# Forty-eight tokens of a PEER kernel's last chunk are taken out of the dense U product, and VectorE's searches, dots and masks are laid out anew around it

## The chip, the cores and the metric

The kernel runs on one NeuronCore of a Trainium2 chip. TensorE (PE) multiplies, VectorE (DVE) and ScalarE (ACT) do element-wise work, GpSimd (POOL) issues the gathers, SyncE (SP) issues most loads. All engines run their own instruction streams and meet at semaphores. The metric is the device time of one execution in microseconds; the kernel before takes 1597.27 us (median of three runs, 1597.15 to 1597.89).

## The reference

512 tokens of 1024 channels go through a gated short-convolution and pooling mixer, then through a PEER layer, which is where the change lies:

```python
q = (xf @ w_query).reshape(t, 8, 2, 128)
scores = einsum('thpk,hpnk->thpn', q, sub_keys)       # 8 heads, 2 halves, 128 keys
v1, i1 = top_k(scores[:, :, 0], 16)
v2, i2 = top_k(scores[:, :, 1], 16)
cand = v1[..., :, None] + v2[..., None, :]
best, pos = top_k(cand.reshape(t, 8, 256), 16)
experts = e1 * 128 + e2                                # 128 experts for a token, of 16384
gates = softmax(best)
a = gelu(einsum('cd,ced->ce', x, expert_u[experts])) * gates
out = einsum('ce,ced->cd', a, expert_v[experts])
```

All is float32 at the borders. The kernel makes each float32 product from three products of float32r parts (high by high, high by low, low by high), which is the origin of the names `w_hi`, `w_lo`, `xn_hi`, `xn_lo`.

## The kernel before, in words

**Tiles.** All weights come as tiles of 128 x 1024 numbers (512 KB), 344 in all: 32 for the input projection, 4 for the pool, 32 for the gates, 8 for `w_out`, 16 for the query, 128 for U, 128 for V. Four slots hold them. SP loads `w_raw` once the slot's `w_lo` is done, ACT makes `w_hi` (`split_weight`, L683) once PE has finished the tile four places earlier, DVE makes `w_lo` (L1272), PE multiplies (`tile_product`, L1019: eight blocks of three matmuls, 24 in all).

**Who computes what in PEER.** The 128 tokens of chunk 0 never enter the dense products: DVE takes their 128 expert rows of U each by gather (POOL, L597, a ring of four 512 KB buffers, one row for each of 128 tokens) and dots them with `x_tok` (L1666), and later adds gated rows of V into `out_tok` (L1895). The last `EXTRA` = 32 tokens of chunk 3 are taken out of the dense U product as well: 128 experts for a token are one more kind of gathered row, with 16 partitions for a token and eight tokens (`SHARED`) in a group (L1673), each row against `x_extra`, which holds a group's x. The other 352 tokens get the dense product of x with all 16384 rows of U: 128 tiles of 24 matmuls with 352 columns (`DENSE`, `DU`). V takes 384 tokens, in matmuls of 512 columns.

**Order in the U stage** (U tiles 0 to 127). While PE multiplies the query tiles and then U tiles, DVE searches the top 16 of each head (`search`, L1544), one chunk and two heads at a call, and decodes expert numbers. Between the pieces of a search stand a few `u_split` (L1534), the DVE step that frees a bank and makes the `w_lo` of the tile four further on (for half of tiles 4 to 39 `w_lo` comes from DRAM and DVE only signals). `hold` between two pieces makes DVE wait until the piece before is written. The tables `SEARCHES`, `DOTS_BEFORE`, `DOTS_ROUND` and `DOTS_PLAIN` (L134 and on) say how many splits and dots stand where. Retrieval ends before the split of U tile 52.

**Masks.** From U tile 60 to 107 run six rounds of eight tiles. In a round DVE writes four mask groups of 16 tokens (`mask_half`, L1803): one 128 x 2048 tensor of e1 lanes and, in the next place, two (three for the `EXTRA` tokens) of gated e2 columns, one group for two tiles, besides one `w_lo` and `DOTS_ROUND` dots for a tile. PE turns them into gates by 128 x 128 products (L1199), half a mask group (16 matmuls) after each tile: it needs mask group n after tile 2n of the stage. The second half of group n is written before the split at tile 2n - 1. ACT copies the results (L878), two groups of four tokens behind each tile, and stores them to `g_dram`, 2 MB for four tiles. Steps 27 to 30 (16 tiles) are plain: U tiles and dots alone. What dots are then left run in the first V tiles; from V tile 37 on, DVE adds 128 rows of V, spread evenly to the end.

The lines that say this most briefly:

```python
DOTS_ROUND = (1, 1, 1, 2, 1, 1, 1, 2)
for q in (2 * b, 2 * b + 1):                      # PE, after u_tile b
    if q % 4 == 0:
        pe.wait_ge(masks_ready, MASKS_PER_ROUND * s + (q // 4 + 1))
if q >= ROW_SLOTS:                                # POOL: the ring of four
    pool.wait_ge(rows_used, q - ROW_SLOTS + 1)
```

Of the kernel before, what the change touches and what calls it, by code (L numbers as in the profile page):

```python
# [75 lines left out]
EXTRA = 32  # L76
# [18 lines left out]
EXP_AT = 54  # L95
# [33 lines left out]
def is_early(step, b):  # L129
# [4 lines left out]
SEARCHES = (((3, 1, 1, 0), 0, 2), ((2, 1, 0, 1), 1, 2), ((2, 1, 1, 0), 0, 2), ((2, 0, 1, 1), 1, 2),  # L134
            ((2, 1, 0, 1), 0, 2), ((1, 1, 1, 0), 2, 2), ((2, 1, 0, 1), 0, 2), ((1, 1, 1, 1), 2, 2),
            ((2, 1, 1, 0), 0, 0), ((2, 1, 0, 1), 2, 0))
BEFORE_FIRST = EXP_AT - 2
DOTS_BEFORE = (1, 1, 1, 2, 1, 1, 1)
DOTS_ROUND = (1, 1, 1, 2, 1, 1, 1, 2)
DOTS_PLAIN = (2, 2, 1, 2)  # L140
DOTS_TOPK = sum(dots for _, _, dots in SEARCHES)
# [4 lines left out]
X_STORED, X_LOADED, X_AT_ONCE = 6, 10, 2  # L146
assert EXTRA_SHOWN + 2 < EXTRA_FIRST and EXTRA % MASKED == 0
# [70 lines left out]
class Chain:  # L218
# [23 lines left out]

    def hold(self, carrier):


        self.wait()
        self.engine.sem_inc(carrier, 1)


def build(nc, x_t, params_d, w_in_d, pool_d, gate_d, w_out_d, query_d, keys_d, u_d, v_d, u_rows, gain_d, out_d,  # L250
          act_dram, g_dram, index_dram, extra_dram, x_rows_dram, early_dram):
    ctx = ExitStack()
    with ctx:
# [71 lines left out]
        top_v = rest("top_v", [P, 2, 2, TOPK])  # L325
        top_i = rest("top_i", [P, 2, 2, 2, 2, TOPK], U32)
        less = rest("less", [P, 4, KEYS])
        cand = rest("cand", [P, 2, CANDS])
        cand_less = rest("cand_less", [P, 2, CANDS])
# [5 lines left out]
        x_last = rest("x_last", [P, D])  # L335
# [4 lines left out]
        extra_t = small("extra_t", [P, EXTRA])  # L340
        extra_rows = small("extra_rows", [P, PAIRS])
        gate_x = small("gate_x", [P, EXTRA_PARTS, EXTRA], BF16)
# [3 lines left out]
        beside_xn = MemoryMap(nc, xn_at)  # L346
        x_extra = [beside_xn(f"x_extra{k}", [P, NB, T])[:, :, 0:GT] for k in range(X_BUFFERS)]
        assert beside_xn.at <= scratch_at
# [19 lines left out]
                 for k, at in enumerate(mask_regions)]  # L368
        masks_x = [MemoryMap(nc, at)(f"masks_x{k}", [P, 1 + EXTRA_PARTS, MASKED // 2, KEYS, 2], BF16)
                   for k, at in enumerate(mask_regions)]  # L370
        g_build.at += 2 * (1 + EXTRA_PARTS) * MASKED * KEYS
# [210 lines left out]
        def _(pool):  # L582
# [30 lines left out]
            def load_extra(t):  # L613

                g, at = t // SHARED, t % SHARED * SPREAD
                pool.dma_start(x_extra[g % X_BUFFERS][at:at + SPREAD],
                               x_rows_dram[t:t + 1, :].broadcast_to([SPREAD, D])
                               ).then_inc(x_extra_loaded[g % X_BUFFERS], 16)
# [15 lines left out]
            for q in range(U_ROWS):  # L634
# [38 lines left out]
        def _(act):  # L673
# [224 lines left out]
            act.activation(act_out[:, :, DU:], ones[:, 0:SLOTS * EXTRA].rearrange("p (b t) -> p b t", b=SLOTS), ACT.Copy  # L898
# [30 lines left out]
            for b in range(SLOTS // 2, SLOTS):  # L929
                gelu_tile(ONEHOT_AT - 1, b)  # L930
# [1067 lines left out]
```

## Time and profile before

| what | value |
|---|---|
| median of three runs | 1597.27 us |
| the profiled execution, its own time | 1597.16 us |
| its span, first to last instruction | 1595.4 us |
| PE busy | 1587.8 us (100%) |
| DVE busy | 1289.7 us (81%) |
| ACT busy | 701.6 us (44%) |
| POOL busy | 426.2 us (27%) |
| granted TensorE clock | full (1.000) |
| DMA moved | 459.85 MB, mean 288 GB/s |

The span in 40 slices shows DVE at 7 or more tenths from the thirteenth slice on, and the DMA engines at 9 tenths from the 20th to the 39th, at 333 to 414 GB/s. The chain that ended last is 98% PE. A matmul's own time in a row is from issue to its last result; matmuls overlap, so the pace is the distance of two starts. VectorE's instructions overlap a little too: 1.22 us for a 128 x 1024 operation, with the next one 1.14 us after its start.

The U stage runs from 521 to 1064 us, the mask rounds in it from 752 to 990 us, the V stage from 1067 to 1590 us.

### The profile page before, as it was taken

To read this page: it belongs to the slowest core of one execution; us is meant where nothing else is said; L and a number is where in the kernel's file an instruction comes from. 1 tells how busy PE (TensorE), PEld (TensorE's weight loads), DVE (VectorE), ACT (ScalarE), POOL (GpSimd) and SP (SyncE) were. 2 spreads that over 40 slices of the span, in tenths; PEclk is the share of its full clock that TensorE was granted. 3 is DMA by queue.
4 is the path that set the end of the run, shared out by engine and by line. 5 is a ranking of instruction groups with operands and counts; after the bars stand their busy time and mean duration, and the time that the engine had idled before them with its cause. 6 is when DMAs were issued, how large, how long until landed. Compare 5 with 4: busy or idle time off the path is not lost.

```text
span 1595.4 us, 25473 instructions
## 1 busy us (share of the span) xinstructions
PE 1587.8 (100%) x8590; PEld 1403.7 (88%) x8590; DVE 1289.7 (81%) x2373; ACT 701.6 (44%) x936; POOL 426.2 (27%) x373
## 2 busy tenths in 40 slices
PE   9999999999999999999999999999999999999998
PEld 8888888888888999999999999998888888888886
DVE  6967833334578888988999998779998999999997
ACT  5444533333333433335776776443334333333334
POOL 1011100000000112203353322434445555455451
PEclk9999999999999999999999999999999999999999
DMA  5477632323322699968999999999999999999994
GB/s 214 143 250 239 234 106 96 101 92 100 111 82 78 231 337 318 325 205 281 333 386 410 406 389 379 407 356 373 390 413 387 413 414 394 410 407 397 404 358 162
DMA packets 150237, 459.85 MB, mean 288 GB/s; under 512 B 16336, under 2 KB 47104, under 8 KB 148512
## 3 DMA queue, kind: packets, MB, share of 16 engines
q1 hardware_dynamic: 82080, 231.08, 39.4%
q0 software_dynamic: 47888, 172.15, 28.5%
q10 hardware_dynamic: 20208, 55.94, 9.3%
q8 instruction: 22, 0.36, 0.1%
q14 instruction: 39, 0.32, 0.1%
HBM read 402.78 MB, written 56.33 MB: 288 GB/s over the span
## 4 chain that ended last, share of the span: by engine, by line
PE 98%; ACT 1%; DVE 1%; DMA 1%; issue 0%; SPq 0%; DVEq 0%; ACTq 0%
PE bank L1036 20%; PE bank L1038 20%; PE bank L1037 20%; PE bank L1223 11%; PE bank L1224 11%; PE bank L1222 11%; PE bank L1199 3%; PE bank L1102 1%; DMA h_t<-x_t 1%; PE bank L1236 0%; ACT w_hi L689 0%; DVE w_lo L1275 0%; PE bank L1081 0%; PE bank L1083 0%; PE bank L1082 0%
## 5 line engine op out<-in xcount | busy, mean ns | idle before, releaser
L689 ACT ACTIVATE w_hi<-w_raw 128x1024 fp32r<-128x1024 f32 x347 | 365.9, 1056 | 349.9 <-PE bank L1224 238.9
L1036 PE MATMUL bank<-xn_hi,w_hi 128*128 128x352 f32 (+1 forms) x1472 | 510.4, 347 | 0.0
L1275 DVE TENSOR_TENSOR w_lo<-w_raw,w_hi 128x1024 fp32r<-128x1024 f32 x329 | 401.6, 1221 | 130.8 <-ACT w_hi L689 126.9
L1037 PE MATMUL bank<-xn_lo,w_hi 128*128 128x352 f32 (+1 forms) x1472 | 504.7, 343 | 0.0
L1038 PE MATMUL bank<-xn_hi,w_lo 128*128 128x352 f32 (+1 forms) x1472 | 504.7, 343 | 0.0
L597 POOL DMA_INDIRECT rows<-u_rows,expert x128 | 152.8, 1193 | 610.3 <-DVE expert L1703 353.9
L1222 PE MATMUL bank<-w_hi,a_hi 128*128 128x512 f32 x768 | 298.8, 389 | 0.0
L1224 PE MATMUL bank<-w_hi,a_lo 128*128 128x512 f32 x768 | 298.8, 389 | 0.0
L1223 PE MATMUL bank<-w_lo,a_hi 128*128 128x512 f32 x768 | 298.8, 389 | 0.0
L1038 PEld LDWEIGHTS bank<-xn_hi,w_lo 128*128 128x128 f32 x1472 | 276.7, 188 | 17.7
L1037 PEld LDWEIGHTS bank<-xn_lo,w_hi 128*128 128x128 f32 x1472 | 276.9, 188 | 17.4 <-issue 0.2
L1036 PEld LDWEIGHTS bank<-xn_hi,w_hi 128*128 128x128 f32 x1472 | 276.7, 188 | 17.3 <-issue 0.2
L597 POOL DMA_INDIRECT rows<-v,expert x128 | 189.6, 1481 | 175.6 <-DVE out_tok L1895 161.9
L1222 PEld LDWEIGHTS bank<-w_hi,a_hi 128*128 128x128 f32 x768 | 144.1, 188 | 30.0
L1224 PEld LDWEIGHTS bank<-w_hi,a_lo 128*128 128x128 f32 x768 | 144.1, 188 | 29.9
L1223 PEld LDWEIGHTS bank<-w_lo,a_hi 128*128 128x128 f32 x768 | 144.1, 188 | 29.9
L1895 DVE SCALAR_TENSOR_TENSOR out_tok<-rows,dots,out_tok 128x1024 f32<-128x1024 f32 x128 | 163.9, 1280 | 6.9 <-DMA rows<-v,expert 3.4
L1666 DVE SCALAR_TENSOR_TENSOR rows<-rows,x_tok 128x1024 f32<-128x1024 f32 x128 | 154.0, 1220 | 17.0 <-DMA rows<-u_rows,expert 16.7
L864 ACT ACTIVATE act_out<-bank 128x352 f32<-128x352 f32 x112 | 52.1, 465 | 210.3 <-PE bank L1038 203.8
L962 ACT ACTIVATE a_hi<-a_f 128x384 fp32r<-128x384 f32 x128 | 66.9, 523 | 77.2 <-DVE a_f L1876 76.9
L878 ACT ACTIVATE g_sb<-bank 128x512 f32<-128x512 f32 x96 | 100.7, 1164 | 0.0
L1882 DVE TENSOR_TENSOR a_lo<-a_f,a_hi 128x384 fp32r<-128x384 f32 x128 | 70.5, 551 | 0.0
(239 smaller groups left out, 1486.1 us busy)
## 6 DMA issues: line engine op xcount, KB each, us to landing
w_raw<-u SPq DMA_DIRECT2D x128, 512.0 KB, 6.7
w_raw<-v SPq DMA_DIRECT2D x128, 512.0 KB, 7.1
g_dram<-g_sb ACTq DMA_DIRECT2D x12, 2048.0 KB, 10.9
g_in<-g_dram SPq DMA_DIRECT2D x84, 256.0 KB, 9.0
act_dram<-act_out ACTq DMA_DIRECT2D x54, 352.0 KB, 5.7
act_in<-act_dram SPq DMA_DIRECT2D x54, 352.0 KB, 8.5
w_raw<-gate SPq DMA_DIRECT2D x32, 512.0 KB, 3.3
w_raw<-w_in SPq DMA_DIRECT2D x31, 512.0 KB, 3.8
```

Source lines behind the costliest of these rows:

```text
L597: pool.indirect_dma_start(out=rows[:, slot, :], out_offset=None, in_=table.rearrange("a p d -> (a p) d"), in_offset=bass.IndirectOffsetOnA ...
L689: act.activation(w_hi[:, slot, :], w_raw[:, slot, :], ACT.Copy).then_inc(hi_done, 1)
L878: act.activation(g_sb[:, k, :, t:t + TOKENS_PER_GROUP].rearrange("p e t -> p t e"), bank[4 + q % SLOTS][:].rearrange("p (t e) -> p t e", e ...
L1036: pe.matmul(out, hi, x_hi, start=k == 0, stop=False)
L1037: pe.matmul(out, hi, x_lo, start=False, stop=False)
L1038: last = pe.matmul(out, lo, x_hi, start=False, stop=k == NB - 1)
L1222: pe.matmul(out, a_h, v_hi, start=False, stop=False)
L1223: pe.matmul(out, a_h, v_lo, start=False, stop=False)
L1224: return pe.matmul(out, a_l, v_hi, start=False, stop=final)
L1275: dve.tensor_tensor(w_lo[:, slot, :], w_raw[:, slot, :], w_hi[:, slot, :].bitcast(F32), ALU.subtract).then_inc(lo_done, 1)
L1666: dve.scalar_tensor_tensor(rows[:, slot, :], rows[:, slot, :], 1.0, x_tok[:], ALU.mult, ALU.mult, accum_out=dots[:, r:r + 1]).then_inc(row ...
L1895: dve.scalar_tensor_tensor(out_tok[:], rows[:, slot, :], dots[:, ds(r)], out_tok[:], ALU.mult, ALU.add).then_inc(v_rows_used, 1)
```

## The change

- **Tokens.** `EXTRA` is 48 instead of 32. The dense U product takes 336 columns instead of 352, six instead of four groups of eight tokens go by gathered rows (16 more rows, 176 instead of 160), and three instead of two mask groups have three parts.
- **Searches.** `search` takes two chunks. Each piece is issued for chunk s = 0 and then for s = 1, and `hold_at` waits on the mark of the same chunk's piece before. Retrieval ends before the split of U tile 44 instead of 52.
- **x of the row dots.** `x_extra` is a contiguous 128 x 1024 tensor, loaded by one DMA for a group of eight tokens instead of eight DMAs of one token each into a tensor with gaps (512-byte pieces).
- **Mask groups.** PE takes all 32 matmuls of a group (48 with three parts) after every second tile instead of 16 after every one: it needs group n after tile 2n + 1. ACT copies four groups of four tokens after every second tile.
- **Dots.** 10 in retrieval (16 before), 22 from there to the masks (8), 11 in each of six rounds (10), 28 in the plain steps (28), 50 in V (48). The sum is 176 (160). Rows of V begin at V tile 41 instead of 37. The three turning products of e1, e2 and gates come after U tile 51 instead of 57.

```diff
-EXTRA = 32
+EXTRA = 48
-MASKS_X = EXTRA // MASKED
+MASKS_X = -(-EXTRA // MASKED)
+THREE_PARTS = MASKED * MASKS_X
-DOTS_BEFORE = (1, 1, 1, 2, 1, 1, 1)
-DOTS_ROUND = (1, 1, 1, 2, 1, 1, 1, 2)
+DOTS_FIRST = 1
+DOTS_SEARCH = (1, 1, 1, 2)
+DOTS_DECODE = (1, 1, 1, 1)
+BEFORE_FIRST = 44
+DOTS_BEFORE = (1, 1, 1, 2, 1, 2, 1, 1, 2, 1, 2, 1, 1, 2, 2, 1)
+DOTS_ROUND = (1, 1, 2, 1, 1, 2, 1, 2)
...
+            def load_extra(g):
+
+                pool.dma_start(x_extra[g % X_BUFFERS][:],
+                               x_rows_dram[g * SHARED:(g + 1) * SHARED, :].unsqueeze(1).broadcast_to([SHARED, SPREAD, D])
+                               ).then_inc(x_extra_loaded[g % X_BUFFERS], 16)
...
+                kind, r = u_row(q + SHARED - ROW_SLOTS)
+                if kind and r % SHARED == 0 and r >= X_BUFFERS * SHARED:
+                    load_extra(r // SHARED)
...
-                    for q in (2 * b, 2 * b + 1):
+                    for q in range(2 * (b - 1), 2 * (b + 1)) if b % TILES_PER_MASK == TILES_PER_MASK - 1 else ():
...
+            def mask_groups(s, n, last_round):
+                pe.wait_ge(masks_ready, MASKS_PER_ROUND * s + (n + 1))
+                for q in range(SLOTS * n, SLOTS * (n + 1)):
+                    pe.wait_ge(g_copied, GROUPS_PER_ROUND * s + (q + 1))
...
+                    if b % TILES_PER_MASK == TILES_PER_MASK - 1:
+                        mask_groups(s, b // TILES_PER_MASK, last_round)
...
-            def search(c, i, at, splits):
+            def search(chunks, i, splits):
...
+                for s in both:
+                    for k, u, half in rows_of:
+                        chain.did(dve.max(top_v[:, s, half, u, 0:8], row(s, k)))
+                    done[s] = chain.mark()
+                for s in both:
+                    chain.hold_at(done[s], held)
+                    for k, u, half in rows_of:
+                        chain.did(dve.max_index(index(s, half, u)[:, 0:8], top_v[:, s, half, u, 0:8], row(s, k)))
+                        chain.did(dve.match_replace(less[:, s, k, :], top_v[:, s, half, u, 0:8], row(s, k), LOWEST))
+                    done[s] = chain.mark()
+                    splits[s]()
```

**VectorE at the start of a search.** Before: one chunk (MAX finds eight of the largest, x4 is four calls; `w_lo` is the split of a weight tile).

```order
L1554 MAX top_v<-scores 128x8 x4
L1557 MAX_INDEX top_i<-top_v,scores 128x8
L1558 MATCH_REPLACE less<-top_v,scores 128x128
L1557 MAX_INDEX top_i<-top_v,scores 128x8
L1558 MATCH_REPLACE less<-top_v,scores 128x128
L1557 MAX_INDEX top_i<-top_v,scores 128x8
L1558 MATCH_REPLACE less<-top_v,scores 128x128
L1557 MAX_INDEX top_i<-top_v,scores 128x8
L1558 MATCH_REPLACE less<-top_v,scores 128x128
L1275 TENSOR_TENSOR w_lo<-w_raw,w_hi 128x1024
L1562 MAX top_v<-less 128x8 x4
L1565 MAX_INDEX top_i<-top_v,less 128x8 x4
```

VectorE of the changed kernel, in the second part of a search's first half:

```order
L1576 MATCH_REPLACE less<-top_v,scores 128x128
L1289 TENSOR_TENSOR w_lo<-w_raw,w_hi 128x1024
L1582 MAX top_v<-less 128x8 x8
L1587 MAX_INDEX top_i<-top_v,less 128x8 x4
L1590 TENSOR_TENSOR cand<-top_v 128x2x64
L1590 TENSOR_TENSOR cand<-top_v 128x2x48
L1587 MAX_INDEX top_i<-top_v,less 128x8 x4
L1590 TENSOR_TENSOR cand<-top_v 128x2x64
```

Eight MAX of two chunks stand together, and the second chunk's four lie between the first chunk's four and the operation that reads them.

**TensorE in the first mask round.** Before, after a U tile:

```order
L1038 MATMUL bank<-xn_hi,w_lo 128x352
L1190 ISA
L1191 ISA
L1199 MATMUL bank<-masks_127 128x128 x8
L1191 REGISTER_ALU
L1199 MATMUL bank<-masks_127 128x128 x8
L1026 REGISTER_ALU
L1036 MATMUL bank<-xn_hi,w_hi 128x352
```

TensorE in the first mask round of the changed kernel, after the second U tile:

```order
L1050 MATMUL bank<-xn_hi,w_lo 128x336
L1192 ISA
L1194 ISA
L1202 MATMUL bank<-masks_124 128x128 x8
L1194 REGISTER_ALU
L1202 MATMUL bank<-masks_124 128x128 x8
L1194 REGISTER_ALU
L1202 MATMUL bank<-masks_124 128x128 x8
L1194 REGISTER_ALU
L1202 MATMUL bank<-masks_124 128x128 x8
L1038 REGISTER_ALU
L1048 MATMUL bank<-xn_hi,w_hi 128x336
```

Thirty-two mask products stand in a row where there were sixteen, and one U tile more lies ahead of them.

**GpSimd beside the row gathers.** Before (16x8x128 is one token's x):

```order
L597 DMA rows<-u_rows,expert_extra 128x1024 x12
L616 DMA x_extra_118<-x_rows_dram 16x8x128 x2
L597 DMA rows<-u_rows,expert_extra 128x1024
L616 DMA x_extra_118<-x_rows_dram 16x8x128 x2
L597 DMA rows<-u_rows,expert_extra 128x1024
```

GpSimd of the changed kernel at the same place:

```order
L613 DMA rows<-u_rows,expert_extra 128x1024 x12
L631 DMA x_extra_128<-x_rows_dram 128x1x1024
L613 DMA rows<-u_rows,expert_extra 128x1024 x8
L631 DMA x_extra_129<-x_rows_dram 128x1x1024
```

One load of 512 KB stands ahead of eight gathers where eight loads of 64 KB stood between them.

## Rows read from the trace of the kernel before

**Rows 1.** The page, part 1: engine, busy us (share of the span), instructions.
```profile
PE 1587.8 (100%) x8590; PEld 1403.7 (88%) x8590; DVE 1289.7 (81%) x2373; ACT 701.6 (44%) x936; POOL 426.2 (27%) x373
```

**Rows 2.** Waits of TensorE, whole span: us in total, times, longest.
```profile
PE bank L1058 <- POOL p_pad L585: 1.0, 1, 1.0
```

**Rows 3.** Timeline of TensorE in the U stage: start us, us, instruction.
```profile
599.70 0.32 PE L1036 MATMUL bank<-xn_hi,w_hi 128*128 128x352 f32 x1
...
603.54 0.32 PE L1036 MATMUL bank<-xn_hi,w_hi 128*128 128x352 f32 x1
```

**Rows 4.** Timeline of TensorE in the V stage.
```profile
1199.76 0.39 PE L1222 MATMUL bank<-w_hi,a_hi 128*128 128x512 f32 x1
...
1203.84 0.39 PE L1222 MATMUL bank<-w_hi,a_hi 128*128 128x512 f32 x1
```

**Rows 5.** Chain that ended last, beside the first mask products: start us, us.
```profile
756.85 0.94 PE bank L1199 x16
757.79 0.21 PE bank L1036
```

**Rows 6.** Chain that ended last, a group with three parts.
```profile
969.69 1.40 PE bank L1199 x24
```

**Rows 7.** Timeline of VectorE in a search.
```profile
703.73 0.88 DVE L1554 MAX8 top_v<-scores 128x8 f32<-128x128 f32 x4
704.75 0.09 DVE L1557 MATCH_VALUE_LOAD top_i<-top_v,scores 128x8 f32 x1
```

**Rows 8.** Waits of VectorE while it searches, 445 to 728 us.
```profile
DVE w_lo L1275 <- ACT w_hi L689: 15.1, 11, 3.1
```

**Rows 9.** Timeline of VectorE in a mask round.
```profile
884.43 0.42 DVE L1755 TENSOR_TENSOR low_hot<-iota_key,e_low 128x512 f16<-128x512 f16 x1
...
887.77 2.35 DVE L1775 TENSOR_TENSOR masks<-gated_hot,low_hot 128x2048 f16<-128x2048 f16 x2
...
902.59 0.41 DVE L1755 TENSOR_TENSOR low_hot<-iota_key,e_low 128x512 f16<-128x512 f16 x1
```

**Rows 10.** Timeline of ScalarE at one U tile.
```profile
749.21 0.47 ACT L864 ACTIVATE act_out<-bank 128x352 f32<-128x352 f32 x1 [1.90 <-PE bank L1038]
749.57 1.05 ACT L689 ACTIVATE w_hi<-w_raw 128x1024 fp32r<-128x1024 f32 x1
```

**Rows 11.** Waits of VectorE in the mask rounds, 752 to 990 us.
```profile
DVE w_lo L1275 <- ACT w_hi L689: 7.7, 19, 2.9
DVE rows L1673 <- DMA rows<-u_rows,expert_extra: 5.0, 4, 2.5
```

**Rows 12.** Waits of VectorE in the plain steps, 990 to 1064 us.
```profile
DVE rows L1666 <- DMA rows<-u_rows,expert: 14.5, 13, 2.7
```

**Rows 13.** Stretches: us, busy us of each engine (instructions), PEclk, DMA share, GB/s.
```profile
752.00:990.00 238.00, 238.00 (x1980) 231.62 (x1979) 224.48 (x296) 165.10 (x196) 81.67 (x75) 1.00 1.00 381
990.00:1064.00 74.00, 74.00 (x466) 73.98 (x465) 56.91 (x81) 31.32 (x56) 35.26 (x30) 1.00 1.01 399
...
1230.00:1560.00 330.00, 330.00 (x1458) 273.25 (x1457) 313.27 (x361) 126.83 (x163) 171.90 (x117) 1.00 1.02 400
```

**Rows 14.** DMA issues, 752 to 990 us: count, KB each, us to landing.
```profile
rows<-u_rows,expert POOLq DMA_INDIRECT x31, 9.8
rows<-u_rows,expert_extra POOLq DMA_INDIRECT x28, 11.6
```

**Rows 15.** DMA issues, 1230 to 1560 us.
```profile
rows<-v,expert POOLq DMA_INDIRECT x117, 7.4
```

**Rows 16.** Timeline of VectorE in the V stage.
```profile
1314.87 2.67 DVE L1895 SCALAR_TENSOR_TENSOR out_tok<-rows,dots,out_tok 128x1024 f32<-128x1024 f32 x2
1317.45 0.56 DVE L1876 TENSOR_TENSOR a_f<-act_in,g_in 128x384 f32<-128x384 f32 x1
...
1319.52 1.28 DVE L1895 SCALAR_TENSOR_TENSOR out_tok<-rows,dots,out_tok 128x1024 f32<-128x1024 f32 x1
1320.72 0.55 DVE L1876 TENSOR_TENSOR a_f<-act_in,g_in 128x384 f32<-128x384 f32 x1
```

More of the change, by code:

```diff
@@ L94 @@
 ONEHOT_AT = 15
-EXP_AT = 54
+TURN_AT = 13
 ROUND = 2
@@ new lines, in search @@
+                for s in both:
+                    chain.hold_at(done[s], held)
+                    for k, u, half in rows_of:
+                        chain.did(dve.max(top_v[:, s, half, u, 8:16], less[:, s, k, :]))
+                    done[s] = chain.mark()
+                for s in both:
+                    chain.hold_at(done[s], held)
+                    for k, u, half in rows_of:
+                        chain.did(dve.max_index(index(s, half, u)[:, 8:16], top_v[:, s, half, u, 8:16], less[:, s, k, :]))
+                    for first, count, width, start in ((0, TOP_A, TOPK, 0), (TOP_A, TOPK - TOP_A, LOW_B, WIDE)):
+                        part = [P, 2, count, width]
+                        chain.did(dve.tensor_tensor(
+                            cand[:, s, :, start:start + count * width].rearrange("p u (a b) -> p u a b", a=count),
+                            top_v[:, s, 0, :, first:first + count].unsqueeze(3).broadcast_to(part),
+                            top_v[:, s, 1, :, 0:width].unsqueeze(2).broadcast_to(part), ALU.add))
+                    done[s] = chain.mark()
+                    splits[2 + s]()
@@ new lines, in search @@
+                for s in both:
+                    chain.hold_at(done[s], held)
+                    for u in range(2):
+                        chain.did(dve.max(top(s, u)[:, 0:8], cand[:, s, u, :]))
+                    done[s] = chain.mark()
+                for s in both:
+                    chain.hold_at(done[s], held)
+                    for u in range(2):
+                        chain.did(dve.max_index(place(s, u)[:, 0:8], top(s, u)[:, 0:8], cand[:, s, u, :]))
+                        chain.did(dve.match_replace(cand_less[:, s, u, :], top(s, u)[:, 0:8], cand[:, s, u, :], LOWEST))
+                    done[s] = chain.mark()
@@ new lines, in search @@
+                splits[4]()
+                for s in both:
+                    chain.hold_at(done[s], held)
+                    for u in range(2):
+                        chain.did(dve.max(top(s, u)[:, 8:16], cand_less[:, s, u, :]))
+                    done[s] = chain.mark()
+                splits[5]()
+                for s in both:
+                    chain.hold_at(done[s], held)
+                    for u in range(2):
+                        chain.did(dve.max_index(place(s, u)[:, 8:16], top(s, u)[:, 8:16], cand_less[:, s, u, :]))
```

304 lines of the change are left out of this document (131 added, 173 removed).

## The prediction

> **What bounds the kernel now.** Read the busy times first: PE is busy for the whole span [rows 1], and the longest of its three waits is 1.0 us, at the very start [rows 2]. So the time is PE's own sum, and nothing else counts until PE waits for it. The second look is for PE's pace. In the U stage 24 starts take 3.84 us, 160 ns for a matmul of 352 columns [rows 3]; in V 18 starts take 4.08 us, 226.7 ns for 512 columns [rows 4]. The third look is for who is close behind PE: in the mask rounds DVE is busy 224.5 of 238 us, in V 313.3 of 330, and the DMA engines are full in both (share 1.00 and 1.02) [rows 13]. That is where a faster PE runs into something.
>
> **PE's own sum.** The two paces differ by 66.7 ns for 160 columns, 0.417 ns a column. Sixteen columns fewer: 6.67 ns, 153.3 ns a matmul, and for 128 tiles x 24 = 3072 matmuls 20.5 us less. The third mask part for 16 more tokens is 16 products of 1.40/24 = 58 ns [rows 6]: 0.9 us more. The first U matmul behind mask products takes 0.21 instead of 0.16 us on the chain [rows 5]; there are 24 such places instead of 48: 1.2 us less. PE's sum is 20.8 us less. The profiled execution took 1597.16 us (1.8 us outside its span), the median is 0.1 above it: 1576.5 if PE never waits. Gathers and DVE must serve a PE that is faster, with 16 rows more; so each stage is looked at.
>
> The weight load could be a floor here: at 352 columns PEld is busy for 73.98 of 74 us [rows 13], and then narrower matmuls win nothing. Against it: from 352 to 512 columns the pace grows by just one column each 2.4 GHz cycle, at the full granted clock, which a floor that held at 352 would bend; and mask products follow each other in 58 ns, loads included, though of 16 bit. The Trainium skill (TensorE: Matmul & The Clock Gate, section "LDWEIGHTS (loading the stationary operand)") gives the load as columns over 1.2 GHz, 107 ns for 128. By it there is no floor at 153 ns and the 20.5 us stand; no row here shows a 32-bit load as a bound.
>
> **Retrieval** (445 to 728 us). It now ends 8 tiles earlier, and 44 U tiles are 0.16 us shorter: DVE has 8 x 3.84 + 44 x 0.16 = 37.8 us less. It saves 8 `w_lo` of 1.14 (9.1) and 6 dots of 1.15 (6.9). A `hold` costs about 0.22 us: four MAX end at 704.61, and the next starts at 704.75, and loses the 0.08 overlap that it would have had [rows 7]. Of seven in a search some four have no `w_lo` in front; paired, all are covered: 16 x 4 x 0.22 = 14. Sum 30; the other 8 come from the 15.1 us in which DVE waits for `w_hi` [rows 8]. It fits with 7 us in hand; cost 0, and up to 8 if the pairs save only half.
>
> **From retrieval to the masks.** 16 tiles x 1.14 + 22 x 1.15 = 43.5 us, and about 9 for the gates and mask group 0 (an estimate from operations as in [rows 9]), in 58.9 us of PE. It fits, but the gates and group 0 (about 6 us) come in one piece near the end, so DVE enters the rounds some 3 us behind (estimate, 0 to 6).
>
> **Mask rounds.** Half a round of DVE without a wait took 902.59 - 884.43 = 18.16 us [rows 9], a round 36.3, with an eleventh dot 37.5. PE's round was 8 x (3.84 + 0.94 + 0.05) = 38.6 and becomes 8 x (3.68 + 0.94) + 0.2 = 37.2. So DVE, which had 2.3 us a round to spare, now lacks 0.3: 2 us in six rounds, and 2 more for the third part of one more group (one operation of 1.14 [rows 9] and its small ones). Gathers: the ring of four must turn in 4/11 of 37.2 = 13.5 us (15.4 before). A row of `expert_extra` lands 11.6 us after its issue, the others 9.8 [rows 14]; with dot and issue 13.1 and 11.3. Spare is 0.4 us where it was 2.3, and with 2.3 DVE lost 5.0 us in four waits [rows 11]. I take 8 us; 0 if the single `x_extra` loads lighten the queue, 20 if landings grow by a microsecond. What is allowed: DVE can begin a split 1.5 us after PE's tile (ACT's 1.4 [rows 10] and a signal). Mask group n stands before split 2n - 1 and PE asks for it after tile 2n + 1, two tiles and a group of products later: 7.36 + 1.87 - 1.5 = 7.7 us of room (3.3 in the order before). 3 + 2 + 2 + 8 = 15 against 7.7 gives 7; some gather waits fall where DVE would wait for `w_hi` anyway (7.7 us of that now [rows 11]), so I take 4, from bounds of 0 and 16.
>
> **Plain steps.** 28 dots and 16 `w_lo` are 50.4 us, row waits 14.5 [rows 12]: 65 us against PE's 58.9. DVE falls 6 us further behind, having won back 3.4 at the two places of the last round that have no masks; room is three tiles less 2.7, 8.3 us. I take 2 us, from 0 to 6.
>
> **V.** The other steps take 1319.52 - 1317.45 = 2.07 us, one row 1.20, a pair 2.58 [rows 16]. 128 rows over 86 tiles instead of 90 are 1.49 a tile: 2.07 + 1.87 = 3.94 us of 4.08 (3.85 before). The ring may take 10.97 us and takes 7.4 [rows 15] + 1.6. Cost 0, while landings stay.
>
> Sum: -20.8 + 4 + 2 = -14.8, that is **1582.5 us**.
>
> **Rivals.**
> *All is covered.* `x_extra` in one piece makes short packets go away, landings shorten, DVE stays inside its room: waits under 3 us, 1577. For it: room in the masks more than doubles. Against: the ring's 0.4 us.
>
> *The DMA engines set the pace.* The stretch of the masks moved 238 us x 381 GB/s = 90.7 MB at a share of 1.00, the plain one 74 x 399 = 29.5 [rows 13]. Six rows and an x group add 3.7, the narrower `act_out` takes 0.5 off: 93.9 MB in 238 - 8 = 230 us are 408 GB/s, then 29.5 in 71.4 are 413. Seen over such lengths are 381 to 400. If the masks stay at 381, they take 246.5 us, 16.5 longer than PE needs: 1576.5 + 16 = 1592.5. For it: the full share. Against: 400 in V at the same share, so share alone is no ceiling. The Trainium skill (DMA: Bandwidth & Descriptors, section "Where 436 GB/s comes from") puts the fabric's ceiling at 435 GB/s, by which 413 passes, and gives about 358 for one core's HBM; the 400 of the rows is above that one already.
>
> *Slower: the ring of V.* Two more dots run in V, and the 128 rows of V crowd into 86 tiles. From a landing of 9.4 us on, the ring turns slower than 10.97 and the whole V stage follows it. At 10.3 us, between this and what the mask rounds show for gathers [rows 14], it turns in 11.9: 32 x 11.9 = 381 us where 351 are given, 30 us more: 1612. For it: mask rounds show 9.8 to 11.6 at the same share. Against: V asks for hardly more bytes, and its row landed in 7.4.
>
> *Nothing is won.* A floor of the weight load: 128 tiles as long as now, 1597.
>
> **Chances.** Forecast 0.52 (1579.5 to 1587), all covered 0.22, DMA pace 0.14, no gain 0.04, slower 0.08. This kernel's measurement can tell about 0.2%, 3.2 us, from no change. Faster 0.52 + 0.22 + 0.13 = 0.87, same 0.05, slower 0.08. The range 1576 to 1593 leaves out the slower case, the floor and the worse half of the DMA case, some 0.19.
>
> **What the new profile should show.** Starts of U matmuls 153.3 ns apart (160 or more would be the floor). 24 groups of 32 or 48 mask products, the row behind at 0.21. PE's waits: next to none before 752 us, some 4 us for `masks` or `w_lo` in the rounds, the later the more, 2 in the plain steps, none in V. DVE at 97% or more in the rounds, its waits for `w_hi` there gone and those for rows of `expert_extra` near 8 us. Retrieval over at about 690 us. The forecast is wrong if PE waits in retrieval or V, if DVE keeps waiting for `w_hi` in the rounds, or if landings move by more than a microsecond either way.

## The result: slower by 1.7%, and the profile after

The changed kernel takes 1622.65 us (median of four runs, 1620.14 to 1631.82) against 1597.49 for the kernel before: a ratio of 1.0168, 95% interval 1.0148 to 1.0188. Forecast were 1582.5 us, and slower had a chance of 0.08. The profiled execution took 1620.67 us. Its page says of PE, and of all DMA packets:

```profile
PE 1579.9 (98%) x8606; PEld 1394.2 (86%) x8606; DVE 1300.5 (80%) x2411; ACT 701.8 (43%) x936; POOL 443.6 (27%) x365
DMA packets 153534, 467.63 MB, mean 289 GB/s; under 512 B 17296, under 2 KB 48080, under 8 KB 151808
```

PE was busy for the whole span before [rows 1]; now it waits. Its waits over the whole span (us in total, times, longest), beside [rows 2]:

```profile
PE bank L1202 <- DVE masks L1800: 15.1, 7, 4.7
PE bank L1048 <- DVE w_lo L1289: 12.8, 10, 4.7
PE bank L1202 <- DVE masks_x L1800: 2.6, 1, 2.6
```

What PE's own work was forecast to win is there. In the U stage two starts that lie 24 matmuls apart (start, duration):

```profile
785.61 0.32 PE L1048 MATMUL bank<-xn_hi,w_hi 128*128 128x336 f32 x1
789.29 0.32 PE L1048 MATMUL bank<-xn_hi,w_hi 128*128 128x336 f32 x1
```

3.68 us for 24 is 153.3 ns, where [rows 3] had 160. So the loss must be waits. Here is one from its root to PE. First GpSimd's queue, then DVE, then PE, in that stretch (start, duration, and in brackets the idle time before and what ended it):

```profile
775.05 0.66 POOL L631 DMA_DIRECT2D x_extra<-x_rows_dram  x1 [2.90 <-DVE rows L1704]
776.01 1.07 POOL L613 DMA_INDIRECT rows<-u_rows,expert_extra  x1 [0.30 <-issue]
```

```profile
786.00 1.22 DVE L1289 TENSOR_TENSOR w_lo<-w_raw,w_hi 128x1024 fp32r<-128x1024 f32 x1
793.17 1.23 DVE L1704 SCALAR_TENSOR_TENSOR rows<-rows,x_extra 128x1024 f32<-128x1024 f32 x1 [5.95 <-DMA rows<-u_rows,expert_extra]
794.32 2.35 DVE L1800 TENSOR_TENSOR masks<-gated_hot,low_hot 128x2048 f16<-128x2048 f16 x2
```

```profile
796.80 3.59 PE L1202 MATMUL bank<-masks 128*128 128x128 f16 x32 [4.59 <-DVE masks L1800]
800.15 0.63 PE L1048 MATMUL bank<-xn_hi,w_hi 128*128 128x336 f32 x1
800.58 0.48 PE L1049 MATMUL bank<-xn_lo,w_hi 128*128 128x336 f32 x1
...
808.08 2.01 PE L1202 MATMUL bank<-masks 128*128 128x128 f16 x32
```

The gather issued at 776.01, right behind a 512 KB load of `x_extra`, feeds the dot of 793.17: 17.2 us, where [rows 14] had 11.6. DVE stands still for 5.95 us, its masks are late, and PE waits 4.59 us for them. Then comes a second price: the same 32 mask products take 3.59 us instead of 2.01, and the U starts behind them are 0.43 and 0.28 us apart instead of 0.153. The granted clock in those stretches (columns as in [rows 13]):

```profile
796.00:800.00 4.00, 3.20 (x31) 3.21 (x32) 4.00 (x5) 2.13 (x3) 0.59 (x2) 0.50 0.84 276
804.00:808.00 4.00, 4.00 (x28) 3.96 (x26) 4.00 (x6) 1.40 (x2) 1.14 (x1) 1.00 1.00 417
```

0.50 is the lower level, 1.2 GHz, right behind a wait; it is back at 2.4 GHz a few us later. The wait cost 4.59 us. Of the 6.9 us at half clock around it (794.3 to 801.2) PE was busy for 4.40, so the slow start cost about half of that, 2.2 us more.

Every wait of over 3 us has this root. The loads for groups 2 to 5 are issued at 745.70, 775.05, 809.43 and 842.49; the first or second gather behind each reached its dot after 15.0, 17.2, 15.3 and 15.6 us, and PE's waits of 4.72, 4.59, 4.75 and 3.78 us follow. The loads of groups 0 and 1 stand ahead of the first extra rows:

```profile
691.94 0.69 POOL L631 DMA_DIRECT2D x_extra<-x_rows_dram  x1 [0.59 <-DVE rows L1697]
...
700.60 0.66 POOL L631 DMA_DIRECT2D x_extra<-x_rows_dram  x1 [0.57 <-DVE rows L1697]
```

Between 698 and 766 us DVE waits 21.0 us for rows, 10.9 of them for the three issued between and behind these two loads (at 698.31, 701.57 and 706.17), and comes late into the mask rounds. Its waits for rows over the whole span were 5.0 and 16.7 us before:

```profile
DVE rows L1704 <- DMA rows<-u_rows,expert_extra: 30.0, 11, 7.4
DVE rows L1697 <- DMA rows<-u_rows,expert: 29.6, 23, 5.6
```

The sum closes. V began at 1067.05 us before and begins at 1090.56 now, 23.5 us later, the whole difference of the spans. PE's own sum was 1576.5; its eighteen waits in the U stage are 15.1 + 12.8 + 2.6 = 30.5 us; what is left to 1620.7 is 13.7 us. The clock was at half in five stretches of the U stage, one at each of the five longest waits (4.72, 4.59, 4.75, 3.78 and 2.57 us):

```profile
763.60:770.50 6.90, 4.80 (x17) 4.80 (x18) 6.90 (x10) 1.79 (x3) 5.60 (x3) 0.51 0.79 252
794.30:801.20 6.90, 4.40 (x36) 4.41 (x37) 6.90 (x11) 4.04 (x5) 2.28 (x2) 0.51 0.86 307
831.90:835.30 3.40, 3.40 (x32) 3.40 (x30) 3.28 (x5) 3.00 (x4) 0.61 (x1) 0.50 0.99 407
866.00:869.50 3.50, 3.50 (x24) 3.50 (x21) 3.47 (x8) 3.35 (x4) 0.90 (x1) 0.51 0.82 314
982.10:985.50 3.40, 3.40 (x36) 3.40 (x34) 3.37 (x7) 2.64 (x3) 0.86 (x1) 0.50 0.96 340
```

PE was busy for 19.5 us in them (second column), of which half, 9.8 us, is the price of the clock. The other 3.9 us are restarts. Around the wait of 1.14 us that ends at 1040.95 us, at full clock, two starts lie 1.46 us apart, 0.17 more than the wait and a step of 0.15, and the next step is 0.26. That is some 0.27 us ahead of each of ten U tiles and 0.17 ahead of each of eight mask groups, 4.1 us by this estimate.

### The profile page after: what moved, and what is told of

Its sections match the earlier page's. It is cut to its first block, busy times and chain, and to the rows that moved or that the text cites. A ratio compares the mean times of both kernels' runs of the same rounds, so it can differ in the third digit from the quotient of the medians.

```text
span 1618.9 us, 25557 instructions
## 1 busy us (share of the span) xinstructions
PE 1579.9 (98%) x8606; PEld 1394.2 (86%) x8606; DVE 1300.5 (80%) x2411; ACT 701.8 (43%) x936; POOL 443.6 (27%) x365
## 2 busy tenths in 40 slices
DMA packets 153534, 467.63 MB, mean 289 GB/s; under 512 B 17296, under 2 KB 48080, under 8 KB 151808
## 4 chain that ended last, share of the span: by engine, by line
PE 72%; DMA 11%; DVE 11%; issue 5%; POOL 1%; ACT 1%; SPq 0%; DVEq 0%; POOLq 0%; ACTq 0%
PE bank L1048 13%; PE bank L1049 13%; PE bank L1050 13%; PE bank L1238 11%; PE bank L1236 11%; PE bank L1237 11%; DMA rows<-u_rows,expert_extra 5%; DMA rows<-u_rows,expert 5%; DVE w_lo L1289 2%; DVE rows L1704 2%; DVE rows L1697 2%; DVE masks L1800 2%; POOL rows L613 1%; PE bank L1114 1%; DVE masks L1791 1%
## 5 line engine op out<-in xcount | busy, mean ns | idle before, releaser
L1048 PE MATMUL bank<-xn_hi,w_hi 128*128 128x336 f32 (+1 forms) x1472 | 504.1, 342 | 12.8 <-DVE w_lo L1289 12.8
L1050 PE MATMUL bank<-xn_hi,w_lo 128*128 128x336 f32 (+1 forms) x1472 | 498.6, 339 | 0.0
L1049 PE MATMUL bank<-xn_lo,w_hi 128*128 128x336 f32 (+1 forms) x1472 | 498.6, 339 | 0.0
L613 POOL DMA_INDIRECT rows<-u_rows,expert x128 | 161.8, 1264 | 653.1 <-DVE expert L1730 371.2
L875 ACT ACTIVATE act_out<-bank 128x336 f32<-128x336 f32 x112 | 50.5, 451 | 205.0 <-PE bank L1050 182.2
L889 ACT ACTIVATE g_sb<-bank 128x512 f32<-128x512 f32 x96 | 95.5, 1157 | 10.5 <-PE bank L1202 10.5
L613 POOL DMA_INDIRECT rows<-u_rows,expert_extra x48 | 60.2, 1254 | 112.7 <-DVE rows L1704 92.5
```

Of the source, the lines that this page charges most:

```text
L613: pool.indirect_dma_start(out=rows[:, slot, :], out_offset=None, in_=table.rearrange("a p d -> (a p) d"), in_offset=bass.IndirectOffsetOnA ...
L889: act.activation(g_sb[:, k, :, t:t + TOKENS_PER_GROUP].rearrange("p e t -> p t e"), bank[4 + q % SLOTS][:].rearrange("p (t e) -> p t e", e ...
L1048: pe.matmul(out, hi, x_hi, start=k == 0, stop=False)
L1049: pe.matmul(out, hi, x_lo, start=False, stop=False)
L1050: last = pe.matmul(out, lo, x_hi, start=False, stop=k == NB - 1)
```

## The experiments

At first three theories stood against each other: a load in one piece is a burst in front of the gathers (burst); sixteen partitions read the same row of DRAM (hot rows); or DVE has too much to do (budget).

**e1_by_token.** The loads again token by token, 64 KB each:

```
-  x_extra[g % 2][:] <- x_rows_dram[8 g : 8 g + 8].unsqueeze(1).broadcast_to([8, 16, D])   # once a group
+  x_extra[g % 2][at:at + 16] <- x_rows_dram[t:t + 1].broadcast_to([16, D])                # for each of 8 tokens, two ahead of a gather
```

> The kernel after, with one edit: x_extra is loaded token by token again (64 KB each, two ahead of a gather, four ahead of each of two gathers for group 0), in place of one 512 KB load ahead of one gather. In the kernel after, every long wait of PE between 760 and 870 us comes behind a gather that was issued right behind such a load and landed after 14.7 to 17.2 us. Theory A (burst): what delays those gathers is the 512 KB in one piece in front of them on the queue. Spread over four gathers nothing waits long: landings 11 to 13 us, PE waits under 10 us in all and no clock loss, 1582 to 1592 us. Theory B (hot rows: 16 partitions read the same 4 KB row of DRAM at once, and that is slow however it is issued): the same slow reads, only spread, 1600 to 1615. Theory C (DVE's budget: eleven dots a round and the third mask part; the loads don't matter): 1617 to 1625.

Measured: 1610.4 us (ratio 1.0073, 1.0055 to 1.0090). Half of the loss goes; the gathers behind loads that DVE has to wait for reach their dots in 9 to 12 us, one in 15.5. The time is outside the burst theory's range and inside the hot rows'. So the form of the kernel before is better here than one load in one piece, by 12.2 us, but it is 12 us worse than the best form found below (e10).

**e2_copies_in_dram.** Sixteen copies of each row in DRAM, so that a load reads 128 rows one after the other:

```
-  x_rows_dram <- x_last[P - EXTRA:]
+  x_rows_dram.rearrange("(t s) d -> t s d", s=16) <- x_last[P - EXTRA:].unsqueeze(1).broadcast_to([EXTRA, 16, D])
-  x_extra <- 8 rows, broadcast to [8, 16, D]
+  x_extra <- x_rows_dram[128 g : 128 g + 128]
```

> The kernel after, with x_rows_dram holding each of the 48 rows 16 times (one 3 MB store during retrieval), so that the single 512 KB load of a group reads 128 different rows of DRAM instead of 8 rows 16 times each. Theory A (burst): the same bytes stand in front of the same gathers, landings of 14.5 to 17 us stay, 1615 to 1630 us. Theory B (hot rows): the load becomes as quick as a gather, the gathers behind it land in 12 to 13.5 us, PE's waits halve or better: 1590 to 1605. Theory C (DVE's budget): as after, 1617 to 1625. The store itself may cost up to 2 us in retrieval in all three.

Measured: 1609.9 us (1.0071, 1.0055 to 1.0088). Its PE waits:

```profile
PE bank L1203 <- DVE masks L1801: 11.0, 11, 3.0
PE bank L1049 <- DMA w_lo<-early_dram: 9.5, 1, 9.5
```

The same bytes in front of the same gathers, which now reach their dots in 10 to 14 us: it is not the burst. In retrieval PE waits 9.5 us for a tile from DRAM behind the 3 MB store, which landed after 27.5 us; that is this experiment's own.

**e3_no_later_loads.** The loads of groups 2 to 5 are left out (`if False: load_extra(...)`), and DVE does not wait for them.

> The kernel after without the four loads of x_extra for groups 2 to 5: their dots are made with the rows of groups 0 and 1 that lie in the same buffers, so the dots of 32 tokens in the rows are made with other x rows; all other work is the same. Theories A and B: PE's waits of 0.8 to 4.8 us between 765 and 865 (19.4 us) and the time at half clock behind them (some 14 us) go, what is left are the first three waits before 741 us (3.5), masks_x (2.6) and the plain steps (4.6): 1585 to 1592 us. Theory C (DVE's budget): DVE was late by its own work, 1612 to 1622.

Measured: 1600.3 us (1.0013, 1.0003 to 1.0023). The four loads cost 22 us. What is left above the forecast, 18 us, has waits of PE too: three waits before 741 us (3.5), 6.7 for masks, 2.9 for `masks_x`, 5.7 in the plain steps.

**e4_before_burst.** The kernel before, its eight small loads in a row ahead of one gather:

```
-  if SHARED <= r < EXTRA - SHARED and r % SHARED >= ROW_SLOTS:   two loads
+  if SHARED <= r < EXTRA - SHARED and r % SHARED == ROW_SLOTS:   all eight loads
```

> The kernel before, with its eight 64 KB loads of a later group of x_extra issued in a row ahead of one gather instead of two ahead of each of four gathers. Only groups 2 and 3 are loaded so in the rounds. Theory A (burst): two gathers behind the loads land after 15 to 17 us instead of 12.8 to 14.3, DVE waits 3 to 5 us behind each, PE's room there is 3.3 us: 1598 to 1606 us, with a PE wait of 1 to 4 us behind one or both. Theory B and theory C: 1596.5 to 1598, no wait of PE.

Measured: 1598.0 us (1.0001, 0.9992 to 1.0011). One row came 4.1 us late for DVE and PE waited 0.4. No burst effect that reaches the time.

**e5_copies_six_stores, e6_copies_ten_dots, e7_copies_by_token.** The 3 MB store cut into six, `[8, 16, D]` each; and with it ten dots a round (`DOTS_ROUND = (1, 1, 1, 2, 1, 1, 1, 2)`), or loads by token as in e1.

> As e2_copies_in_dram (single loads of 128 different rows of DRAM), with the 3 MB store cut into six pieces of 512 KB, one ahead of each of six gathers in retrieval. In the run with one store, PE waited 9.5 us in retrieval for w_lo from early_dram, behind that store. If this was the store's doing, it goes and what is left is the price of the rest: 1599 to 1602 us. If it was not: 1608 to 1612.

> As e5_copies_six_stores, with ten dots a round instead of eleven (56 dots left for V instead of 50). Budget theory (what is left is DVE's: a round of 37.5 us and row waits against PE's 37.2): DVE's round falls to 36.3 us, PE's small waits for masks, one each half round, go, with masks_x perhaps: 6 to 9 us less than e5, 1591 to 1595 us. Entry theory (DVE comes into the rounds late and only that shows): the first waits stay, later ones go: 3 us less. DMA theory (the landings set the pace): within 2 us of e5. V may cost up to 4 us through its six more rows, which would show as a PE wait after 1100 us.

> As e5_copies_six_stores, but each group is loaded by token (eight loads of 64 KB, spread as in e1_by_token), each from 16 different rows of DRAM. In e1_by_token the same loads read one row 16 times and the time was 1610. Hot-row theory: as e5 within 3 us, 1597 to 1603. Small-packet theory (what costs is the number of short packets, 128 or 144 for a group in either form of the broadcast): near e1_by_token, 1606 to 1612.

Measured: 1624.3, 1627.4 and 1631.8 us. All three miss, by a cost of their own: the six stores stand in retrieval ahead of what PE needs there, with five to six waits of 1.6 to 4.0 us between 595 and 690 us. (A load of that shape from SBUF takes 12.2 us for 512 KB in e9; the store itself was not measured alone.) They settle nothing of the size of the waits; behind that stretch e6 has 2.3 us of waits for masks where e5 has 10.0 (and 2.4 for ScalarE's copies, where e5 has none), and 9.5 us of waits in V where e5 has none. What e7 was to tell, whether the number of short packets is what costs, stays open here; the packets of e8 answer it below.

**e8_loads_alone, e9_more_loads_alone.** The loads by themselves.

> Loads by themselves; nothing of the reference is computed, its output is the gain alone. GpSimd's queue, one after the other, six times each: (1) 512 KB as 8 rows read 16 times each, (2) 512 KB as 128 different rows, (3) eight loads of 64 KB, a row read 16 times each, (4) a gather of 128 rows, (5) to (7) each of the first three with a gather issued right behind it; then all seven again beside a stream of 512 KB loads from SyncE's queue, four in flight. Hot-row theory: 1 takes longer than 2 by 2 us or more, and 5 than 6 by as much, more beside the stream. Burst theory: 1 and 2 agree within half a microsecond, and so do 5 and 6.

> More loads of x_extra by themselves, as in e8_loads_alone (where 512 KB from 8 rows of DRAM, each read 16 times, took 6.9 us alone and 11.9 beside a stream, and from 128 rows 3.8 and 7.2); nothing of the reference is computed. Six each of: each of 8 rows read 16 times (the kernel's), 16 rows 8 times, 32 rows 4 times, 128 rows once; 8 rows 16 times with the rows in the inner order (partition 8 s + t instead of 16 t + s); from 8 partitions of SBUF, 16 times each; and the store of 48 rows of SBUF once and 4 times each; then all beside a stream of 512 KB loads. If the cost is that one row of DRAM is read many times at once, then the time falls with the copies (32 rows within 0.5 us of 128 rows), the inner order helps as well, and the load from SBUF has none of it. If it is the number of repeats in the descriptors and not the rows, then only 128 rows are quick, and 32 rows take over 6 us.

Measured, start to next start, medians of six, alone and beside the stream: 8 rows x 16 repeats 6.9 and 11.9 us; 128 rows 3.8 and 7.2; eight loads by token 6.0 and 11.4; a gather 4.9 and 7.9; with a gather right behind, alone, the slow load 9.2, the quick one 6.5 and eight by token 8.9. In e9: 8 x 16 again 7.0 and 11.1; 16 rows x 8 repeats 4.6 and 8.9; 32 rows x 4 repeats 3.7 and 7.3; 16 repeats x 8 rows 4.7 and 9.0; from SBUF as 8 x 16 12.2 and 13.0. Two stretches of e8 beside the stream, the slow loads and the quick ones (columns: length, POOL busy, clock, DMA share, GB/s):

```profile
282.00:350.00 68.00, 3.57 (x6) 1.00 1.01 271
351.00:395.00 44.00, 3.23 (x6) 1.00 1.00 382
```

The DMA engines are full in both, and move 271 or 382 GB/s. So the slow load is a property of its form: 4.7 us later beside other traffic, and the other traffic suffers. Eight loads by token are hardly better; GpSimd spends 3.8 to 3.9 us issuing them, one after the other. That fits the 12 us which e1 stays behind the best form; no run separates it.

**e10_four_copies, e11_forty_tokens.** Four copies of a row in DRAM, loads of 32 rows x 4 repeats; and with it 40 tokens and ten dots a round.

```
+  COPIES = 4
-  x_rows_dram[g * SHARED:(g + 1) * SHARED].unsqueeze(1).broadcast_to([SHARED, SPREAD, D])
+  x_rows_dram[g * 32:(g + 1) * 32].unsqueeze(1).broadcast_to([32, 4, D])
 e11:  EXTRA = 40;  DOTS_ROUND = (1, 1, 1, 2, 1, 1, 1, 2);  extra_t of the 8 tokens between is set to one
```

> The kernel after, with each of the 48 x rows stored four times in DRAM (one 0.75 MB store in retrieval, 6.8 us alone) so that a group's single load reads 32 rows four times each; by itself that load was as quick as one of 128 rows (3.7 and 7.3 us against 7.0 and 11.1). If the rows read 16 times are what the loads cost, the time falls as far as without the later loads (1600.3 us) and a little further, since the first two loads are quick as well: 1596 to 1602 us, the gathers behind a load landing in 10 to 14 us, PE's wait of 9.5 us behind the 3 MB store gone. If the number of repeats or the burst counts in the kernel, it stays above 1610.

> As e10_four_copies, but 40 tokens in row dots instead of 48 and ten dots a round instead of eleven (48 dots left for V). PE: 3072 matmuls 3.33 ns longer than with 48 tokens, 10.2 us more. Budget theory (what is left of PE's waits, some 20 us, comes of DVE and the ring of gathers being asked for more than they give): eight dots and gathers fewer, the waits in the rounds fall under 4 us, no clock loss behind them: 1588 to 1594 us, faster than the kernel before. If the waits come from elsewhere (entry, third mask part, plain steps), they stay and it is 1603 to 1610.

Measured: e10 1598.5 us (1.0013, 1.0000 to 1.0026), 24.1 us less than the changed kernel; e11 1592.0 us (0.9967, 0.9954 to 0.9980), faster than both kernels. The gather behind a load in e10, and its dot 12.3 us later:

```profile
764.28 0.57 POOL L633 DMA_DIRECT2D x_extra<-x_rows_dram  x1 [2.90 <-DVE rows L1708]
765.16 1.14 POOL L614 DMA_INDIRECT rows<-u_rows,expert_extra  x1 [0.31 <-issue]
```

```profile
777.47 1.23 DVE L1708 SCALAR_TENSOR_TENSOR rows<-rows,x_extra 128x1024 f32<-128x1024 f32 x1 [1.03 <-DMA rows<-u_rows,expert_extra]
```

PE's waits in e10, then in e11:

```profile
PE bank L1206 <- DVE masks L1804: 6.5, 9, 1.5
PE bank L1052 <- DVE w_lo L1293: 4.0, 7, 1.1
PE bank L1206 <- DVE masks_x L1804: 2.9, 1, 2.9
```

```profile
PE bank L1208 <- DVE masks L1806: 3.1, 2, 1.7
```

From 752 to 1000 us e10 moves 398 GB/s where the changed kernel moved 373:

```profile
752.00:1000.00 248.00, 238.46 (x2014) 233.57 (x2012) 232.68 (x316) 167.39 (x203) 95.53 (x73) 0.99 1.01 398
```

**e12_forty_one_copy, e13_four_copies_ten_dots, e14_thirty_two.**

> As e11_forty_tokens (1592.0 us), but with one copy of the x rows in DRAM as in the kernel after: the loads of x_extra read 8 rows 16 times each again. If a slow load costs PE's time only where DVE and the ring of gathers have nothing to spare, most of its 5 us is now absorbed (ten dots a round leave DVE about a microsecond a round, the order of the masks 7.7 us of room) and only the first two, ahead of the rounds, show: 1593 to 1598 us. If it costs in any case: three loads in the rounds and two before them at 3 to 5 us each, with half clock behind the waits, 1604 to 1612.

> As e10_four_copies (48 tokens, 1598.5 us), with ten dots a round in place of eleven and 56 instead of 50 left for V. Budget theory: PE's waits for masks and masks_x (9.4 us) and the clock lost behind them (some 4 us) go, as in e6_copies_ten_dots, but DVE is late by up to 9 us at the end of V: U's stage ends 11 to 13 us earlier, the whole is 1592 to 1598 us. If the waits in the rounds are the mask order's or the third part's, they stay, and with V's it is 1603 to 1608.

> As e10_four_copies, with 32 tokens in row dots as before the change and ten dots a round (40 left for V); what stays of the change are the mask groups in one go, the paired searches, the earlier end of retrieval, 22 dots from retrieval to the masks and the single loads (of four copies). PE's sum is that of before less 24 transitions of 0.05 us: 1596.0 us. If these parts cost PE no wait: 1595.3 to 1597 us. If one of them has a price of its own (a wait for masks behind groups of 32 products, a late search): 1599 or more, with PE's waits at its place.

Measured: e12 1612.2 us (1.0085, 1.0071 to 1.0099), 20.2 more than e11 for five slow loads: room in DVE's budget does not absorb them, my guess was wrong. e13, 1604.2 us (1.0040, 1.0026 to 1.0054), misses the budget theory's range too. The waits for masks and `masks_x` fall from 9.4 to 2.6, but PE now waits 3.0 us for the gates that ScalarE copies, and U ends only 3.7 us earlier, not 11 to 13. And DVE is late in V:

```profile
PE bank L1240 <- DVE a_lo L1918: 8.8, 5, 6.7
```

e14 takes 1596.6 us (0.9995, 0.9986 to 1.0004), no PE wait behind retrieval: the mask groups in one go, the paired searches and the earlier end of retrieval cost nothing, and PE's sum for them was right within 0.6 us.

**e15_shapes_alone, e16_order_16_8, e17_forty_order_16_8.** Is it the row that is read 16 times, or the outer dimension of 8?

```
-  x_rows_dram[8 rows].unsqueeze(1).broadcast_to([8, 16, D])      # partition 16 t + s
+  x_rows_dram[8 rows].unsqueeze(0).broadcast_to([16, 8, D])      # partition 8 s + t, index and way back the same
```

> Loads alone again, nothing of the reference is computed. Six each of 512 KB as: 8 rows x 16 repeats; 128 different rows as 8 x 16 (a gap behind each 16); 128 different rows as 16 x 8; 16 repeats x 8 rows; 16 rows x 8 repeats; then the first, second and fourth and 32 rows x 4 repeats with a gather right behind; all nine again beside a stream of 512 KB loads. Width theory (an outer dimension of 8 puts the load on 8 of the 16 DMA engines): 128 different rows as 8 x 16 take 7 us like the slow one, as 16 x 8 they take 3.8. Row theory (one row of DRAM read many times): both take 3.8 us, and only the forms with repeats are slower.

> The kernel after (48 tokens, eleven dots, one copy in DRAM), with the tokens of a group in the inner order of the partitions (8 s + t instead of 16 t + s), in the loads of x_extra, in the index and in the way back of the dots. Each load is still one DMA that reads 8 rows 16 times each, now with 16 as its outer dimension. Width theory: as e10_four_copies or a little more (by itself this form takes 4.7 us against 3.7): 1598 to 1604 us. Row theory: as the kernel after, 1615 to 1625.

> As e12_forty_one_copy (40 tokens, ten dots, one copy, 1612.2 us) with the same order 16 x 8. Width theory: as e11_forty_tokens with four copies, 1591 to 1595 us, faster than the kernel before and without its store of copies. Row theory: 1608 to 1614.

Measured alone in e15 (medians of six): 8 rows x 16 repeats 6.8 us; 128 different rows as 8 x 16 6.6; 128 different rows as 16 x 8 4.9; 16 repeats x 8 rows 4.8; 16 rows x 8 repeats 4.7. Two issues of the second form, 6.68 us apart, then two of the third, 4.84 apart:

```profile
45.44 0.58 POOL L66 DMA_DIRECT2D x_load<-u_rows  x1 [6.09 <-DMA x_load<-u_rows]
52.12 0.58 POOL L66 DMA_DIRECT2D x_load<-u_rows  x1 [6.11 <-DMA x_load<-u_rows]
...
84.59 0.52 POOL L66 DMA_DIRECT2D x_load<-u_rows  x1 [5.80 <-DMA x_load<-u_rows]
89.43 0.52 POOL L66 DMA_DIRECT2D x_load<-u_rows  x1 [4.32 <-DMA x_load<-u_rows]
```

Not one row is read twice there, and the load is as slow as the kernel's; forms of one shape agree, whatever they repeat. Row theory falls. It is the shape. Alone, in e8, six slow loads and then six quick ones, each stretch in 40 equal slices (first row: busy tenths of all 16 DMA engines, second: GB/s):

```profile
DMA  3955400045550033553004255400254510045552
GB/s 156 357 180 160 135 20 0 0 119 147 123 123 12 0 46 135 131 127 86 0 0 33 115 131 131 115 0 0 99 156 106 123 41 0 0 54 164 127 123 57
```

```profile
DMA  0098910007980001798000299500065960004985
GB/s 0 0 216 298 380 60 0 0 22 194 365 335 37 0 0 22 149 432 343 8 0 0 67 276 387 209 15 0 0 74 201 410 261 7 0 0 104 268 350 231
```

Apart from the first slices (where SyncE loads as well) the slow loads never get above 5 tenths, at 100 to 160 GB/s; the quick ones reach 9 tenths and over 400. One slow load and one quick one from first packet to last (length, POOL busy, clock, DMA share, GB/s):

```profile
10.30:14.30 4.00, 0.00 (x0) 1.00 0.47 125
44.20:46.00 1.80, 0.00 (x0) 1.00 0.87 278
```

The packets in the trace of e8 say the same one by one. The 4 KB packets of each of the six slow loads are under way for 4.0 to 4.6 us, mostly 8 or 9 at once (2.5 to 4.1 us of it) and never 16; those of the quick ones for 1.9 to 2.0 us, 16 or more at once for 0.6 to 1.2 us of it. The form 16 x 8 in e15 gets to 16 as well. A rival, that short packets are what costs, falls with this. A load of 8 x 16 has 144 packets of 4 bytes beside its 128 of 4 KB, the quick one 16; but their times add up to about 1.1 us, those of the 4 KB packets to some 32, and the engines share both.

In the kernel before, each of the eight small loads is one row to 16 partitions, 16 wide. In the kernel e16 takes 1606.6 us (1.0059, 1.0046 to 1.0072), 16 less than with 8 x 16 and 8 more than with 32 x 4; e17 1597.8 (0.9997, 0.9989 to 1.0006), against 1612.2 and 1592.0 for the same two forms. Both lie between, nearer to the good form, by 8.1 and 5.8 us worse than it and outside what I had expected of the width alone. Loads alone with a gather right behind, beside the stream, give the same order (medians of e15): 8 x 16 14.4 us, 16 x 8 11.5, 32 x 4 10.1. There 16 x 8 keeps a third of what 8 x 16 costs over 32 x 4, in the kernel 8.1 of 24.1 and 5.8 of 20.2 us.

e1 and e2 had both come out in the hot rows' ranges, though that theory is wrong. This was luck: each edit also changed the outer dimension, from 8 to 16 and to 128.

The Trainium skill (DMA: Bandwidth & Descriptors, "Rules for kernel authors") says that an outermost dimension of under 16 confines a whole DMA to at most as many engines. The runs agree: 8 x 16 takes 6.6 to 7.0 us against 3.7 to 3.8, at half the engines' share when alone. It would have given the cause before any run; I had looked at the bytes and packets of this load, not at its shape.

## Why the prediction was wrong, step by step

- **PE's own sum: right.** 153.3 ns a matmul, no floor of the weight load; e14 is at 1596.6 us where the same arithmetic gives 1596.0.
- **Retrieval at no cost, over at 690 us: right.** The index leaves at 688.83 us, and from there back to the start of the U stage PE has no wait; the first comes at 723.
- **Mask rounds, "0 if the single `x_extra` loads lighten the queue, 20 if landings grow by a microsecond": this is the step that failed.** The ring's small reserve of 0.4 us was seen, and that the rows' landings decide; but the load in one piece was priced at zero or below. Gathers behind it landed 3 to 5.6 us later, not 0 to 1. PE's waits in U are 30.5 us instead of 6. Six such loads cost 24.1 us against loads of 32 x 4 (e10 against the changed kernel), five cost 20.2 (e11, e12). Against the loads by token, the form before the change, the merged load costs 12.2 us (e1), about half of the 25.2 us that the change lost.
- **"Short packets go away": false.** Packets under 512 B are 17,296 now. The page of before and that of e16, whose loads differ from the changed kernel's in shape alone:

```profile
DMA packets 150237, 459.85 MB, mean 288 GB/s; under 512 B 16336, under 2 KB 47104, under 8 KB 148512
```

```profile
DMA packets 152766, 467.63 MB, mean 291 GB/s; under 512 B 16528, under 2 KB 47312, under 8 KB 151040
```

The form 8 x 16 adds 768 short packets, 128 a load.

- **From retrieval to the masks, 3 us behind: wrong.** The sum of instructions fitted; the row waits behind the first two loads, 10.9 us of DVE, were no term of it. PE waits 3.5 us for `w_lo` between 723 and 741 us, where next to nothing was forecast before 752; in e10, with quick loads, these waits are gone.
- **A price left out: the clock.** I counted a wait as its length. Here 9.8 us of half clock and some 4 of restarts come on top of 30.5.
- **Budget of DVE and the ring: right in mechanism, too small.** With quick loads (e10) PE waits 6.5 + 2.9 + 4.0 = 13.4 us in the U stage, not 6. Its profiled execution (1596.0 us) is 19.5 us above PE's sum: these 13.4; 2.9 of half clock, from one stretch of 6.8 us with PE busy for 5.8; and some 3 of restarts. Of the 13.4, the eleventh dot's share is in the rounds (2.6 us of waits for masks in e13, and none for `masks_x`), but ten dots only move the work into V.
- **Plain steps 2 us (0 to 6): 4.6, within its range. V at no cost: right** for 50 rows. With 56 (e13) it costs 8.8 us, so it had almost nothing to spare.
- **Rivals.** The slower one had a wrong place (V). The DMA pace of 381 GB/s is none: e10 moved 398 with as many rows. The forecast needed 408 there, and whether full DMA engines hold a part of e10's 13.4 us no run shows. "All is covered" rested on the wrong sign.
- **What the new profile should show.** Right: 153.3 ns, no wait of DVE for `w_hi` in the rounds, none of PE in V. Wrong: DVE is busy for 221.7 of 248 us from 752 on, 89% and not 97, because it waits 26.4 us there for rows of `expert_extra` instead of 8. The last sign named, landings that move by more than a microsecond, is the one that came.

Chances: 0.87 for faster came from cases that all shared the zero for this load.

## What to carry to other kernels

Of a DMA that is merged or reshaped, read the shape before the bytes: `[8, 16, D]` took 6.8 us and held back what stood behind it, `[32, 4, D]` with the same bytes 3.7. A queue that others wait on turns such a delay into PE waits, and a long wait costs more than its length: here the five of 2.6 to 4.8 us, 20.4 us together, cost 9.8 more at half clock. When an edit is costed at nothing or at a gain, put the other sign into the range.

## What the runs showed of the hardware

- 512 KB to 128 partitions alone, by outer dimension of the access pattern: 8: 6.6 to 7.0 us; 16: 4.6 to 4.9; 32: 3.7; 128: 3.8. Beside a stream of 512 KB loads: 11.1 to 11.9; 8.4 to 9.0; 7.3; 7.0 to 7.2. With 8, mostly 8 or 9 packets of 4 KB are under way at once and the engines' share is 0.47 (e8); with 128, 16 or more and 0.87. Why 16 is slower than 32 no run shows.
- Reading a row of DRAM 16 times costs nothing that shows: 4.8 us with repeats and 4.9 without (as 16 x 8), 6.8 and 6.6 (as 8 x 16).
- The same form 8 x 16 read from SBUF takes 12.2 us, beside the stream 13.0.
- With loads of 8 x 16 beside the stream the DMA system is full (share 1.01) at 271 GB/s, with 128 rows it is full (1.00) at 382.
- PE is at half clock (0.50, 1.2 GHz) for 3.4 to 6.9 us at each of the five waits of 2.57 to 4.75 us in the changed kernel, and 32 mask products take up to 3.59 us instead of 2.01. Not every such wait has it: at one of 2.90 us in e5 the clock stays full.
